# Moving the prompt's final mLSTM state from the mLSTM stage of a decoder step into the stage that chooses experts

## The chip, the cores and the metric

The kernel runs on one core of a Trainium2 chip. The metric is device time in microseconds (us); the time before is the median of three executions. The engines are TensorE (PE, matrix multiplication; PEld is its weight load), VectorE (DVE), ScalarE (ACT), GpSimd (POOL) and SyncE (SP), which here only issues transfers. Each engine runs its own instructions in order and waits on semaphores. Transfers run on 16 DMA engines, and each engine that issues transfers has a queue of its own on them: q1 in the profile carries what SP issues, q10 what ACT issues.

## What is computed

One inference step of one decoder layer, for a prompt of 256 tokens and 8 decoding sequences ("samples"), all in float32. The part that matters is the mLSTM with 4 heads of 256 x 256 and its final state for the prompt, then the mixture of experts.

```python
def mlstm_chunk(carry, inp):
    c0, n0, m0 = carry
    q, k, v, i_pre, logf = inp
    ...
    w_end = jnp.exp(F[..., -1:] + a - m_end[..., None])
    c1 = dec_end[..., None, None] * c0 + jnp.einsum('bhs,bhsv,bhsk->bhvk', w_end, v, k)
    n1 = dec_end[..., None] * n0 + jnp.einsum('bhs,bhsk->bhk', w_end, k)
    return (c1, n1, m_end), h
...
h = rmsnorm(x + concat([mlstm, attention]) @ w_out)
# each token: 1 of 4 groups, then 2 of its 8 experts
y = (silu(x_e @ w_gate[e]) * (x_e @ w_up[e])) @ w_down[e]     # 32 experts, 12 MB of weights each
```

`c1` (the memory, prompt_C, 4 heads of 256 KB) and `n1` (the normaliser, prompt_n, 4 rows of 1 KB) of the prompt are outputs. Nothing later in the step reads them.

## The kernel before

The work is laid out by hand in stages. Input projection, attention and mLSTM share one stream of weight chunks of 1 MB (`load_chunk`, `project_chunk`, line 154): the mLSTM stage (`mlstm`) issues 16 such chunks, `project(0)` to `project(15)`, on TensorE and puts the mLSTM's own small matmuls between them. Then comes the choosing stage (`route`): the rest of the output projection, logits, ranks, the gathering of the tokens of expert 0 (`gather_slots`, line 1292), and then `experts`, which takes the 32 experts in order.

The final state before. `weighted_values(h)` on VectorE writes `vw`, the values times `w_end`, for one head; `outer(h)` on TensorE (line 966) multiplies them with the keys in `ktok` into a PSUM bank; `copy_state(h)` on VectorE copies it to `cout`; SP stores it (`prompt_state`, line 869). `normaliser(j)` (line 975) does the same for `n1` with one column of weights, ScalarE copies the row (line 1097) and SP stores it. `outer` and `normaliser` stand between the chunks 7 and 11.

The weights of an expert are six items of 2 MB in a ring of six slots: items 0 and 1 are w_gate, 2 and 3 w_up, 4 and 5 w_down. Slots 0 to 2 are the tile `raw`, slots 3 to 5 the tile `more`; the queue SP loads slot `at` of the next expert when TensorE has used it (`chunk_used`). In `route`, SP loads expert 0 as its slots come free (3, 4, 5, 2, 0, 1), and two more items of expert 1 into other tiles ("extra", line 1476). Slot 2 is `core.raw[:, 4:6]`, and `ktok` and the buffer `hh` of the mLSTM stage are these same two parts of `raw`.

For an expert (line 1879) TensorE does `project(0, 0)`, `project(0, 1)` with slots 0 and 1, `project(1, 0)` with slot 2, `folded(0)`, `project(1, 1)` with slot 3, `folded(1)`, the gathering for the next expert, `down` with slots 4 and 5, and `x_turn`; the first four experts are followed by a piece of another projection (`ple_project`, lines 1333 and 1338). `folded(m)` waits for ScalarE's copy of the PSUM bank (lines 1762 and 1768, `gu_copied`). Ahead of its first such copy ScalarE runs `routing["after"]` (line 1569).

## Time and profile before

| | us |
|---|---|
| median of 3 executions | 1639.27 (1638.75 to 1639.69) |
| span of the profiled execution, first to last instruction | 1635.1 |
| difference of the median to that span | 4.2 |
| TensorE busy | 1355.8 (83%) |
| VectorE, ScalarE, GpSimd busy | 293.3, 226.8, 75.6 |
| traffic | 535.71 MB, mean 328 GB/s |

The profiled execution has no time of its own beside its span. Its parts by time: projections and attention to 313 us, the mLSTM stage from 313 to 459 us, the choosing stage from 459 to 547 us, the experts from 547 to 1478 us, the final stage to 1635 us. A row of the timeline is start, duration, engine, line, operation, output and inputs, count, and in square brackets the idle time of the engine ahead of it with what ended it. A matmul of 32-bit numbers counts as two records on PE.

### The profile page before, as it was taken

The page shows a single profiled execution, that of the slowest core. Times are in us where ns is not written, and L with a number is a line of the kernel's source. Part 1 is how long each engine was busy: PE and PEld are TensorE (multiplying, and loading weights), DVE is VectorE, ACT ScalarE, POOL GpSimd, SP SyncE. Part 2 cuts the span into 40 slices and gives each one's busy share as a digit, 9 for nine tenths or more (in the row PEclk, how much of TensorE's full clock was granted, in tenths as well). Part 3 has the DMA queues.
Part 4 walks back from the last instruction along what each step waited for, and adds up shares of the span by engine and source line. Part 5 has one row for each costly group of instructions (what it writes and reads, how often), then busy time and mean ns, then how long its engine had stood idle before and what let it go on. Part 6 is the DMA issues. An engine that isn't in the chain of part 4 may idle for free.

```text
span 1635.1 us, 21890 instructions
## 1 busy us (share of the span) xinstructions
PE 1355.8 (83%) x9071; PEld 754.3 (46%) x9072; DVE 293.3 (18%) x819; ACT 226.8 (14%) x512; POOL 75.6 (5%) x160
## 2 busy tenths in 40 slices
PE   9999999999999798777777767767677677676997
PEld 7878888888887333222222222222222222223543
DVE  4312321156512301010000100100100000103212
ACT  3101221223211111000000000000000000002303
POOL 1000000200040000000000000000000000000000
PEclk9999999999999799888978988888988887987999
DMA  9555333578886899999999999999999999996352
GB/s 314 176 178 182 129 129 120 185 255 319 266 297 253 357 427 427 428 428 428 428 428 429 428 428 429 427 429 428 428 429 429 428 428 418 425 392 211 105 178 80
DMA packets 106372, 535.71 MB, mean 328 GB/s; under 512 B 13988, under 2 KB 36712, under 8 KB 79945
## 3 DMA queue, kind: packets, MB, share of 16 engines
q1 hardware_dynamic: 101584, 530.56, 81.1%
q0 software_dynamic: 2560, 4.34, 0.7%
q8 instruction: 38, 0.62, 0.2%
q10 hardware_dynamic: 2176, 0.09, 0.1%
q14 instruction: 14, 0.11, 0.0%
HBM read 514.32 MB, written 24.62 MB: 330 GB/s over the span
## 4 chain that ended last, share of the span: by engine, by line
DMA 47%; PE 23%; DVE 1%; ACT 0%; issue 0%; SPq 0%; POOLq 0%; DVEq 0%
DMA raw<-in_w_up 38%; DMA more<-in_w_up 8%; PE ps L2081 7%; PE ps L1854 7%; PE ps L154 4%; PE ps L1292 1%; PE ps L2098 1%; PE ps L1874 1%; PE ps L1333 1%; PE ps L1863 1%; PE ps L1834 1%; DMA more<-expert_rows 0%; DMA expert_rows<-hT,si 0%; PE ps L1493 0%; PE ps L2070 0%
## 5 line engine op out<-in xcount | busy, mean ns | idle before, releaser
L1854 PE MATMUL ps<-raw,hT 128*32 128x512 f32 x1504 | 232.7, 752 | 158.7 <-DMA raw<-in_w_gate 95.6
L154 PE MATMUL ps<-hT,raw 128*128 128x264 f32 x1280 | 291.4, 387 | 0.0
L154 PEld LDWEIGHTS ps<-hT,raw 128*128 128x128 f32 x1280 | 240.8, 190 | 41.9 <-issue 1.5
L1854 PEld LDWEIGHTS ps<-raw,hT 128*32 128x32 f32 x1504 | 46.6, 125 | 310.7 <-DMA raw<-in_w_gate 124.5
L154 PE MATMUL ps<-mixT,raw 128*128 128x264 f32 x640 | 145.5, 387 | 2.4 <-PEq L839 1.5
L1874 PE MATMUL ps<-more,hid 128*32 128x512 f32 x1024 | 125.6, 620 | 21.1 <-DMA more<-in_w_down 21.0
L154 PEld LDWEIGHTS ps<-mixT,raw 128*128 128x128 f32 x640 | 120.8, 190 | 25.0 <-issue 3.9
L1863 PEld LDWEIGHTS ps<-fold,hT 128*128 128x128 f32 x512 | 69.6, 208 | 97.6 <-ACT hT L1768 61.7
L2081 PE MATMUL ps<-raw,more 128*128 128x512 f32 x256 | 114.1, 602 | 0.0
L1810 DVE TENSOR_TENSOR hid<-ps,sig 128x128 f32<-128x128 f32 x32 | 9.3, 291 | 573.3 <-PE ps L1863 573.3
L1292 PE MATMUL ps<-x_res,mine 128*32 128x512 f32 (+1 forms) x792 | 105.5, 649 | 2.2 <-DVE mine L1282 2.2
L1854 PE MATMUL ps<-more,hT 128*32 128x512 f32 x512 | 79.6, 751 | 32.8 <-DMA more<-in_w_up 32.7
L1863 PE MATMUL ps<-fold,hT 128*128 128x32 f32 x512 | 76.7, 295 | 22.9 <-ACT hT L1768 22.9
L1874 PEld LDWEIGHTS ps<-more,hid 128*32 128x32 f32 x1024 | 28.5, 113 | 118.5 <-issue 75.6
L1834 PEld LDWEIGHTS ps<-ident,xe 128*64 128x64 f32 x1056 | 66.8, 217 | 28.5 <-issue 28.5
L1762 ACT ACTIVATE hT<-ps 128x512 f32<-128x512 f32 x32 | 19.1, 597 | 411.4 <-PE ps L1854 411.4
L2081 PEld LDWEIGHTS ps<-raw,more 128*128 128x128 f32 x256 | 48.6, 193 | 57.8 <-issue 57.8
L1834 PE MATMUL ps<-ident,xe 128*64 128x64 f32 x1056 | 71.4, 288 | 0.8 <-ACT xe L1300 0.8
L1818 DVE COPY hT<-ps 128x512 f32<-128x512 f32 x32 | 22.1, 692 | 227.6 <-PE ps L1874 227.6
L1932 POOL DMA_INDIRECT expert_rows<-hT,si x32 | 31.5, 984 | 655.0 <-DVE hT L1818 655.0
L1292 PEld LDWEIGHTS ps<-x_res,mine 128*32 128x32 f32 (+1 forms) x792 | 19.8, 112 | 57.1 <-issue 55.7
L1854 PEld LDWEIGHTS ps<-more,hT 128*32 128x32 f32 x512 | 15.3, 124 | 61.4 <-DMA more<-in_w_up 35.6
(389 smaller groups left out, 793.4 us busy)
## 6 DMA issues: line engine op xcount, KB each, us to landing
more<-in_w_down SPq DMA_DIRECT2D x64, 2048.0 KB, 26.3
raw<-in_w_gate SPq DMA_DIRECT2D x62, 2048.0 KB, 26.3
more<-in_w_up SPq DMA_DIRECT2D x32, 2048.0 KB
raw<-in_w_up SPq DMA_DIRECT2D x32, 2048.0 KB, 26.6
raw<-in_w_in SPq DMA_DIRECT2D x44, 1024.0 KB, 5.1
raw<-in_w_out SPq DMA_DIRECT2D x16, 1024.0 KB, 8.5
raw<-in_w_ple_gate SPq DMA_DIRECT2D x16, 1024.0 KB, 5.0
x_res<-in_state_mlstm_C SPq DMA_DIRECT2D x8, 1024.0 KB, 8.4
```

Source lines behind the costliest of these rows:

```text
L154: return nc.tensor.matmul(ps[:, j, 0:NT], core.raw[:, q % NCH, k * GW + j * P:k * GW + (j + 1) * P], xT[:, core.groups[g].k0 + c * CK + k, ...
L1292: last = nc.tensor.matmul(ps[a * SLOTS:(a + 1) * SLOTS, 2, :], rt["mine"][0:n, t, :], core.x_res[0:n, t, a * GW:(a + 1) * GW], start=(t == ...
L1333: last = nc.tensor.matmul(ps[:, bank[t], :], core.pinT[:, k, t * P:(t + 1) * P], core.wp[:, k, g * GW:(g + 1) * GW], start=(k == 0), stop= ...
L1762: nc.scalar.activation(gu[:, 0, :], ps[:, GATE, :], ACT.Copy).then_inc(q["gu_copied"], 1)
L1818: V.tensor_copy(yq[:], ps[:, YB, :]).then_inc(q["y_copied"], 1)
L1834: last = nc.tensor.matmul(ps[h * 64:(h + 1) * 64, XB, k * 64:(k + 1) * 64], by_row[:, k, :], quarters[:, h], start=True, stop=True)
L1854: last = nc.tensor.matmul(ps[own, (GATE, UP)[m], :], xT[:, k, i * SLOTS:(i + 1) * SLOTS], weights, start=(i == 0 and k < 4), stop=(i == EI ...
L1863: last = nc.tensor.matmul(ps[:, GB, (m * 4 + j) * SLOTS:(m * 4 + j + 1) * SLOTS], gu[:, m, :].rearrange("p (i r k) -> p i k r", i=EI, k=2) ...
L1874: last = nc.tensor.matmul(ps[a * SLOTS:(a + 1) * SLOTS, YB, :], hid[:, 2 * i + k, :], chunk(2 * EI + i)[:, k * D + a * GW:k * D + (a + 1) ...
L1932: pool.indirect_dma_start(out=y4, out_offset=bass.IndirectOffsetOnAxis(ap=si[:, 0:1], axis=0), in_=yq[:], in_offset=None, bounds_check=8 * ...
L2081: last = nc.tensor.matmul(ps[:, 2 * t + g % 2, :], xT[:, c * CK + k, t * P:(t + 1) * P], core.raw[:, c, k * GW:(k + 1) * GW], start=(c == ...
L2098: last = nc.tensor.matmul(ps[a * SLOTS:(a + 1) * SLOTS, 4 + g % 2, 0:P], xsT[:, k, :], core.raw[:, k // CK, k % CK * GW + a * P:k % CK * G ...
```

## The change

The four `outer` and two `normaliser` groups, the copies and the stores leave the mLSTM stage. At its end VectorE writes all eight weighted value tiles into the buffer `hh` (now read as `vw` by `route`) and copies the weights to `core.end_cols`. In `route`, TensorE multiplies head by head (`state(h, b)`) at four places, and the normaliser after the gathering for expert 0, with its four heads in four column groups of the array. ScalarE copies the results to four places in the tile `hT` (`cout`) and to four rows of `pps`, and issues the eight stores itself. SP loads slot 2 for expert 0 (`item(2)`) only after the matmuls have read it. VectorE, GpSimd and ScalarE wait until all eight stores have landed (`r_cstored`, `state_stored`) before they reuse those places: ScalarE at the start of `after`.

```diff
@@ mlstm, tensor
-            project(7)
-            outer(0)
-            project(8)
+            for n in range(7, 12):
+                project(n)
             pe.wait_ge(q["m_den"], 2 * MH)
             pe.wait_ge(q["m_tab2T"], 2)
-            normaliser(0)
-            normaliser(1)
-            outer(1)
-            project(9)
-            outer(2)
-            project(10)
-            outer(3)
-            project(11)
-            pe.wait_ge(q["m_cout"], MH)
-            pe.wait_ge(q["m_nn"], 2)
@@ mlstm, vector, last
+            def weighted_values():
+                dve.wait_ge(q["m_hT"], 8)
+                V.tensor_copy(core.end_cols[:], cols[:, 2])
+                for h in range(MH):
+                    for b in range(2):
+                        V.tensor_scalar(hh[:, b, h, :], vaug[:, b, h, 0:DK], cols[:, 2, b, h:h + 1], None, ALU.mult)
@@ route, sync
         load_chunk(core, sp, first + NCH + 3)
-        item(2)
...
+        sp.wait_ge(q["r_state"], MH)
+        sp.wait_ge(q["r_nT"], 1)
+        item(2)
         sp.wait_ge(shared["xs_clear"], 1)
@@ route, tensor
+        def state(h, b):
+            for v in range(2):
+                last = nc.tensor.matmul(ps[:, state_bank[h], v * DK:(v + 1) * DK], vw[:, b, h, v * P:(v + 1) * P],
+                                        ktok[:, b, h * DK:(h + 1) * DK], start=(b == 0 and v == 0),
+                                        stop=(b == 1), skip_group_check=True)
+            if b == 1:
+                last.then_inc(q["r_state"], 1)
+        def normaliser():
+            for b in range(2):
+                for h in range(MH):
+                    last = nc.tensor.matmul(ps[32 * h:32 * h + 1, 3, 0:DK], core.end_cols[:, b, h:h + 1],
+                                            ktok[:, b, h * DK:(h + 1) * DK], start=(b == 0), stop=(b == 1))
+            last.then_inc(q["r_nT"], 1)
...
+        state(0, 0)
         pe.wait_ge(q["r_const"], 1)
         pe.wait_ge(q["r_l_copied"], 1)
...
         last.then_inc(q["r_pin_turned"], 1)
+        state(0, 1)
+        state(1, 0)
+        state(1, 1)
+        pe.wait_ge(q["r_pin_copied"], 1)
+        state(2, 0)
+        state(2, 1)
         pe.wait_ge(q["r_rank"], 1)
...
+        state(3, 0)
+        state(3, 1)
         gather_slots(core, pe, rt, shared, 0)
+        pe.wait_ge(q["r_c"], 1)
+        normaliser()
@@ route, scalar
+        for h in range(MH):
+            act.wait_ge(q["r_state"], h + 1)
+            nc.scalar.activation(cout[h], ps[:, state_bank[h], :], ACT.Copy).then_inc(q["r_c"], 1)
         slots_copy(core, act, rt, shared, 0)
...
+        act.wait_ge(q["r_nT"], 1)
+        for h in range(MH):
+            nc.scalar.activation(tail["pps"][32 * h:32 * h + 1, 0:DK], ps[32 * h:32 * h + 1, 3, 0:DK], ACT.Copy).then_inc(q["r_n"], 1)
+        act.wait_ge(q["r_c"], MH)
+        for h in range(MH):
+            act.dma_start(out["prompt_C"][0, 0, h].rearrange("(v p) k -> p v k", p=P),
+                          cout[h].rearrange("p (v k) -> p v k", v=2)).then_inc(q["r_cstored"], 16)
+        act.wait_ge(q["r_n"], MH)
+        for h in range(MH):
+            act.dma_start(out["prompt_n"][0, :, h, :], tail["pps"][32 * h:32 * h + 1, 0:DK]).then_inc(q["r_cstored"], 16)
     def after(act):
+        act.wait_ge(q["r_cstored"], 32 * MH)
         act.wait_ge(q["r_wts"], 1)
@@ experts, vector, body
                     slot_index(core, dve, rt, q, p)
+                    dve.wait_ge(*routing["state_stored"])
@@ experts, gpsimd, body
+                    pool.wait_ge(*routing["state_stored"])
                     link(nc.gpsimd.memset(tail["ybs"], 0.0))
```

TensorE's rows in the mLSTM stage, from chunk 7 on, before (L154 are the chunks, L966 `outer`, L975 `normaliser`, L984 the turning of the heads):

```order
L154 MATMUL ps<-hT,raw 128x264 x16
L966 MATMUL ps<-raw,vw 128x256 x4
L154 MATMUL ps<-mixT,raw 128x264 x16
L975 MATMUL ps<-raw,cols 1x256 x8
L966 MATMUL ps<-raw,vw 128x256 x4
L154 MATMUL ps<-mixT,raw 128x264 x16
L966 MATMUL ps<-raw,vw 128x256 x4
L154 MATMUL ps<-mixT,raw 128x264 x16
L966 MATMUL ps<-raw,vw 128x256 x4
L154 MATMUL ps<-mixT,raw 128x264 x16
L984 MATMUL ps<-ident,raw 128x128 x8
```

The same place after the change, from one group further up (L935 is `values`, L944 the turning of the heads):

```order
L935 MATMUL ps<-vaug,gain_row 128x257 x3
L154 MATMUL ps<-hT,raw 128x264 x16
L154 MATMUL ps<-mixT,raw 128x264 x64
L944 MATMUL ps<-ident,raw 128x128 x8
L154 MATMUL ps<-mixT,raw 128x264 x16
```

Chunks 7 to 11 now follow each other with nothing between them: 16 matmuls of `outer` and 8 of `normaliser` are gone from there.

ScalarE's rows at the end of the choosing stage and in expert 0, before (L1300 copies the gathered tokens, L1563 and L1565 are exponentials, L1569 is `after`, L1762 the copy for which `folded(0)` waits):

```order
L1300 ACTIVATE xe<-ps 128x512
L1563 ACT_TABLE_LOAD
L1563 ACTIVATE ra<-ra 128x12
L1565 ACTIVATE rc<-rc 128x3
L1569 ACTIVATE wts<-ps 128x2
L1762 ACTIVATE hT<-ps 128x512
```

and after the change (L1529, L1537 the new copies, L1540, L1544 the new stores, L1742 the copy for `folded(0)`):

```order
L1529 ACTIVATE hT<-ps 128x512 x4
L1231 ACTIVATE xe<-ps 128x512
L1532 ACT_TABLE_LOAD
L1532 ACTIVATE ra<-ra 128x12
L1534 ACTIVATE rc<-rc 128x3
L1537 ACTIVATE pps<-ps 1x256 x4
L1540 DMA out_prompt_C<-hT 128x2x256 x4
L1544 DMA out_prompt_n<-pps 1x256 x4
L1549 ACTIVATE wts<-ps 128x2
L1742 ACTIVATE hT<-ps 128x512
```

Eight copies and eight stores came in, and between the last store and L1549 stands the wait for all eight to have landed.

## Rows read from the trace of the kernel before

**Rows 1.** Page, the chain that ended last, by line.

```profile
DMA raw<-in_w_up 38%; DMA more<-in_w_up 8%; PE ps L2081 7%; PE ps L1854 7%; PE ps L154 4%; PE ps L1292 1%; PE ps L2098 1%; PE ps L1874 1%; PE ps L1333 1%; PE ps L1863 1%; PE ps L1834 1%; DMA more<-expert_rows 0%; DMA expert_rows<-hT,si 0%; PE ps L1493 0%; PE ps L2070 0%
```

**Rows 2.** Windows: stretch, length, busy per engine, clock, DMA share, GB/s.

```profile
380.00:459.00 79.00, 76.36 (x353) 62.97 (x351) 40.88 (x155) 24.60 (x57) 0.00 (x0) 1.00 0.84 291
544.00:546.00 2.00, 1.50 (x25) 1.53 (x26) 0.00 (x0) 1.95 (x4) 0.00 (x0) 0.95 0.97 395
546.00:552.00 6.00, 5.14 (x36) 1.67 (x37) 1.61 (x7) 0.00 (x0) 0.00 (x0) 0.50 0.06 14
552.00:560.00 8.00, 7.44 (x106) 3.10 (x98) 1.25 (x5) 2.71 (x5) 0.19 (x1) 0.96 0.98 383
```

**Rows 3.** Timeline of PE in the mLSTM stage, chunks 7 to 11.

```profile
379.03 7.28 PE L154 MATMUL ps<-hT,raw 128*128 128x264 f32 x32
386.15 1.89 PE L966 MATMUL ps<-raw,vw 128*128 128x256 f32 x8
...
395.09 3.62 PE L975 MATMUL ps<-raw,cols 128*1 128x256 f32 x16
...
407.58 1.89 PE L966 MATMUL ps<-raw,vw 128*128 128x256 f32 x8
...
418.26 1.97 PE L966 MATMUL ps<-raw,vw 128*128 128x256 f32 x8 [1.67 <-DVE vw L1139]
...
427.18 1.04 PE L984 MATMUL ps<-ident,raw 128*128 128x128 f32 x8
```

**Rows 4.** Timelines of DVE and PE, the samples' last values and their user.

```profile
444.12 0.23 DVE L1240 TENSOR_TENSOR nsq<-num 128x64 f32<-128x64 f32 x1
...
450.30 0.53 PE L1041 MATMUL ps<-nsq,ones 128*128 128x32 f32 x4
```

**Rows 5.** Timeline of PE, end of choosing stage and experts 0, 1.

```profile
528.80 0.77 PE L1521 MATMUL ps<-logit_fold,space 128*128 128x36 f32 x6 [1.38 <-DVE space L1595]
...
535.60 0.80 PE L1529 MATMUL ps<-both,upper 128*128 128x128 f32 x2 [4.99 <-DVEq L1624]
...
539.24 4.45 PE L1292 MATMUL ps<-x_res,mine 128*32 128x512 f32 x24 [2.19 <-DVE mine L1282]
544.50 2.21 PE L1834 MATMUL ps<-ident,xe 128*64 128x64 f32 x32 [0.81 <-ACT xe L1300]
...
554.61 1.92 PE L1854 MATMUL ps<-raw,hT 128*32 128x512 f32 x16
556.46 1.13 PE L1863 MATMUL ps<-fold,hT 128*128 128x32 f32 x8
...
564.06 3.64 PE L1874 MATMUL ps<-more,hid 128*32 128x512 f32 x32
...
577.25 1.90 PE L1854 MATMUL ps<-raw,hT 128*32 128x512 f32 x16
```

**Rows 6.** DMA view of 436 to 440 us: SP's queue, and the stores.

```profile
q1 hardware_dynamic: 546, 0.53, 38.1%
...
out_prompt_C<-cout SPq DMA_DIRECT2D x2, 256.0 KB, 2.8
```

**Rows 7.** DMA view of 11 to 20 us: queue, packets, MB, share of 16 engines.

```profile
q1 hardware_dynamic: 1577, 3.13, 98.4%
q10 hardware_dynamic: 1547, 0.05, 12.2%
```

**Rows 8.** DMA view of 800 to 1000 us, SP's queue.

```profile
q1 hardware_dynamic: 5818, 84.77, 99.5%
```

**Rows 9.** Timelines of SP and ACT at expert 0.

```profile
551.27 2.82 SPq L1716 DMA_DIRECT2D raw<-in_w_gate  x2
...
554.78 0.59 ACT L1762 ACTIVATE hT<-ps 128x512 f32<-128x512 f32 x1
```

**Rows 10.** Timeline of PE in the final stage, after an idle stretch.

```profile
1494.06 5.62 PE L2081 MATMUL ps<-raw,more 128*128 128x512 f32 x8
...
1499.95 3.60 PE L2081 MATMUL ps<-raw,more 128*128 128x512 f32 x8
```

More of the change, by code:

```diff
@@ L811, in mlstm @@
     skq = spare[0:NS, 0:2 * MH * DK].rearrange("p (i c) -> p i c", i=2)
-    nout = spare[0:1, 2 * MH * DK:3 * MH * DK].rearrange("p (h k) -> p h k", h=MH)
     vaug = S("vaug", [P, 2, MH, DK + 1])
     kq = S("kq", [P, 2, 2, MH * DK])
-    vw = S("vw", [P, 2, DK])
-    cout = S("cout", [P, 2, 2, DK])
     n0 = S("n0", [NS, MH, DK])
@@ L912, in _ @@
                 load_chunk(core, sp, n)
-            for i in range(2):
-                sp.wait_ge(q[f"m_cst{i}"], 16 * (MH // 2))
-            sp.wait_ge(q["m_stored"], 64)
+            sp.wait_ge(q["m_stored"], 48)
             sp.wait_ge(q["m_cstored"], 16 * NS)
@@ L955, in values @@
                 last.then_inc(q["m_num"], 1)
-            def outer(h):
-                if h == 0:
-                    pe.wait_ge(q["m_wt"], MH)
-                if h >= 2:
-                    pe.wait_ge(q["m_cout"], h - 1)
-                for b in range(2):
-                    pe.wait_ge(q["m_vw"], 2 * h + b + 1)
-                    for v in range(2):
-                        last = nc.tensor.matmul(ps[:, 4 + h % 2, v * DK:(v + 1) * DK], vw[:, b, v * P:(v + 1) * P],
-                                                ktok[:, b, h * DK:(h + 1) * DK], start=(b == 0 and v == 0),
-                                                stop=(b == 1), skip_group_check=True)
-                last.then_inc(q["m_c"], 1)
-            def normaliser(j):
-                for h in (2 * j, 2 * j + 1):
-                    for b in range(2):
-                        last = nc.tensor.matmul(ps[0:1, 6 + j, (h % 2) * DK:(h % 2 + 1) * DK], cols[:, 2, b, h:h + 1],
-                                                ktok[:, b, h * DK:(h + 1) * DK], start=(b == 0), stop=(b == 1))
-                last.then_inc(q["m_nT"], 1)
             def heads(j):
@@ L1094, in _ @@
             decay(4)
-            for j in range(2):
-                act.wait_ge(q["m_nT"], j + 1)
-                nc.scalar.activation(nout[:, 2 * j:2 * j + 2, :], ps[0:1, 6 + j, :].rearrange("p (h c) -> p h c", h=2),
-                                     ACT.Copy).then_inc(q["m_nn"], 1)
             partial(0)
@@ L1353, in ple_copy, with route @@
         nc.scalar.activation(dst, src, ACT.Copy).then_inc(shared["pp_copied"], 1)
-def route(core, w, part, mixT, rt, shared, ctx):
+def route(core, w, out, part, mixT, rt, shared, ctx):
     nc, ps = core.nc, core.ps
@@ L1393, in route @@
     first = core.first_chunk[first_group]
+    vw = core.raw[:, NCH, :].rearrange("p (b h k) -> p b h k", b=2, h=MH)
+    ktok = core.raw[:, NCH + 1, :].rearrange("p (b c) -> p b c", b=2)
+    flat = part[:].rearrange("p k t -> p (k t)")
+    cout = [flat[:, c:c + 2 * DK] for c in (1536, 2560, 3072, 3584)]
+    state_bank = (3, 7, 1, 4)
     def pool(pool):
@@ L1657, in vector @@
         dve.sem_inc(q["r_wt"], 1)
-    return {"pool": pool, "sync": sync, "tensor": tensor, "scalar": scalar, "vector": vector, "extra": extra, "tables": tables, "after": after, "wp_landed": q["r_wp"],
+    return {"pool": pool, "sync": sync, "tensor": tensor, "scalar": scalar, "vector": vector, "extra": extra, "tables": tables, "after": after, "wp_landed": q["r_wp"], "state_stored": (q["r_cstored"], 32 * MH),
             "pin_copied": q["r_pin_copied"], "free": oT}
@@ L2333, in build @@
             shared = dispatch_sems(core)
-            routing = route(core, w, hT, mixT, rt, shared, s)
+            routing = route(core, w, out, hT, mixT, rt, shared, s)
             last = tail_stage(core, w, rt, routing["free"], ydram, out["y_prompt"], out["y_sample"])
```

39 lines of the change are left out of this document (5 added, 34 removed).

## The prediction

> **What bounds the kernel now.** I read the chain that ended last first [rows 1]: nearly half of it is "DMA in_w_up", the wait for expert weights, and the rest is TensorE. So there are two regimes, and a change has to be judged at the border. The windows give it [rows 2]: in the mLSTM stage (380 to 459 us) TensorE is busy 76.4 of 79 us; in 552 to 560 us the 16 DMA engines are busy 0.98 and stay so through the experts (in 800 to 1000 us SP's queue alone fills 99.5%, 84.77 MB [rows 8]). From 552 us on, the end is therefore "traffic still to be moved, plus gaps". One load of 2 MB costs 2.097 MB / (84.77 MB / 200 us) = 4.95 us there. Just ahead of it lies a hole: in 546 to 552 us the DMA engines are busy 0.06 and in 544 to 546 us 0.97, so 5.7 us are idle, because every slot is full until expert 0 has used slot 0 (SP's next load is issued at 551.27 [rows 9]). A microsecond saved on TensorE ahead of 546 us moves everything behind it by one; anything after that counts only if it adds traffic or opens a gap in it.
>
> I keep the clock of the kernel before for all times below and subtract the first saving at the end.
>
> **Step 1, what leaves the mLSTM stage.** From the first `outer` at 386.15 to the turning of the heads at 427.18 are 41.03 us [rows 3]. They hold four chunks; a chunk takes 386.15 - 379.03 = 7.12 us. So 41.03 - 4 x 7.12 = 12.5 us go: four `outer` groups of 1.9 us, the normaliser's 3.6 us and a stall of 1.67 us on a weighted value. Do the other engines follow? The tightest follower is VectorE, whose samples' values end at 444.35 for a matmul at 450.30 [rows 4], 5.9 us of slack. The steps ahead of them are paced by ScalarE behind the chunks and move along; VectorE also loses its waits on stores. Its eight new weighted values come after its last step, beside TensorE's last chunk of 7.12 us; at about 0.4 us each (an estimate; a copy of twice the size takes ScalarE 0.59 [rows 9]) they are hidden there. DMA is busy 0.84 of 79 us [rows 2], 66.4 us, less 3.0 us for the stores that leave (0.381 x 4 us for two of them is 1.52 us [rows 6]): 63.4 us of work in 66.5 us. That is tight but fits, and a chunk's load is issued as soon as the chunk four ahead of it is used. I take **-12.5 us**, bounds -11 and -12.5 with a stall.
>
> **Step 2, the matmuls in the choosing stage.** `state(0, 0)` is half an `outer`, 0.95 us, in a wait of 1.38 us ahead of 528.80; `state(0, 1)` to `state(2, 1)` are 4.7 us in a wait of 4.99 us ahead of 535.60; `state(3)` is 1.9 us in one of 2.19 us ahead of 539.24 [rows 5]. All are covered, just. The normaliser's 16 records follow the gathering. Before, in one column group, 16 cost 3.6 us [rows 3]; the gathering runs 24 records of twice the columns in four groups in 4.45 us at the low clock [rows 5], so four groups cost 4.45 x 16/24/2 = 1.5 us, against a wait of 0.81 us for the gathered tokens: at most 0.7 us late on `x_turn`. In the other direction, the granted clock in 546 to 552 us is 0.50, the level of 1.2 GHz [rows 2], after TensorE had waited three times; filled waits may keep the 2.4 GHz and save some 3 us on the gathering and the first two projections. Neither decides anything, as step 3 shows: behind 546 us the queue, not TensorE, is full. I count 0.
>
> **Step 3, what the DMA engines get to do at the border.** Slot 2's load (4.95 us) used to run earlier in the choosing stage, beside TensorE's chunks; it is now issued at about 543 to 546 us, after the normaliser. The four stores add 3.0 us in the same place. Both fall in the hole of 5.7 us, so the traffic is +7.95 - 5.7 = +2.3 us longer there, if nothing else waits.
>
> **Step 4, the new wait of ScalarE.** In order behind it stand the copy of `wts`, then the copy of expert 0's gate bank at 554.78 [rows 9], for which `folded(0)` waits at 556.46 [rows 5], and behind that all of expert 0 and every free slot after the third. So I need the moment when the eight stores have landed. On an idle queue one store lands 2.8 us after its issue [rows 6], and issued at 546 to 549 us they would be just in time. But they are on ACT's queue q10 while SP's q1 is full. How two queues share shows at the start of the kernel: in 11 to 20 us q1 moved 1577 packets and q10 1547, one for one, though q1's were 2 KB and q10's 32 bytes, and q1 filled the engines all the while [rows 7]. The turn is by packet, not by size. A store here is 256 packets of 1 KB (546 packets for two stores and little else [rows 6]), four are 1024 or 64 per engine. Expert weights are 84.77 MB / 5818 = 14.6 KB per packet [rows 8], in the main 16 KB, 8 per load and engine. So each 1 KB of state waits for 16 KB of weights. From 546.2 us q1 holds slot 2, then slots 0 and 1 of expert 2 and slot 2 of expert 1, as TensorE frees them up to `project(1, 0)`: 4 x 8 = 32 packets per engine, fewer than 64. The stores thus get half of their turns, q1 runs dry because TensorE stands at `folded(0)`, and the rest rushes through: landed at 546.2 + 4 x 4.95 + 3.0 = **569 us**. With ScalarE's two copies TensorE goes on at about 570.5, 14 us later than 556.46.
>
> The Trainium skill (DMA: Bandwidth & Descriptors, section "Queues, rings and completion order") says that a DMA engine round-robins between queues packet by packet, a packet being some 9 to 17 descriptors. The trace agrees on the one-for-one turn; if the turn is a store's 16 rows against a load's 8, the four stores still need four loads' time, and the same 569 us comes out.
>
> **Step 5, the gaps.** After 14 us idle TensorE restarts slowly, as at 1494.06, where 8 records take 5.62 us instead of 3.60 [rows 10]; I give `folded(0)` and `project(1, 1)` (1.13 + 1.92 us) 5.7 us. Slot 3 is free at 576.2, and 0.8 us pass from issue to traffic (551.27 to 552 [rows 2, 9]): DMA idle 569.0 to 577.0, **8.0 us**. That load ends at 581.9; slot 4 is free after ScalarE's copy (0.6 and a pass 0.1), `folded(1)` 1.1, gathering 2.9 and half of `down` 1.8 [rows 5], at 582.7: idle **1.6 us**. Slots 4 and 5 fill to 593.4. Slot 2 of expert 1 is free 577.25 + 1.90 - 561.2 = 17.9 us after the end of `folded(1)` [rows 5], at 595.9: idle **3.3 us**. After that loads stay ahead. Gaps 12.9 us against the old hole of 5.7.
>
> **Sum.** -12.5 + 4.95 + 3.0 + 12.9 - 5.7 = +2.7 us. On the profiled span 1635.1 that is 1637.8, with the 4.2 us outside it **1642 us**. The saving is real and is given back at the border.
>
> **Rivals.**
> - *The stores get through at once.* If q10 may move several packets per turn against one of 16 KB, or the shares go by bytes, they land by about 552, ScalarE is hardly late, and only step 3 remains: -12.5 + 2.3 = -10.2, 1629 us. For it: 3.0 us of traffic is little; 2.8 us landing on an idle queue. Against: 1577 to 1547.
> - *Partly.* Two or three packets per turn: landed at 558 to 563. Up to about 558 the loads already queued cover ScalarE's lateness; each later us costs about one. 1632 to 1638, say 1636 us.
> - *Slower, by the mLSTM stage.* 63.4 us of traffic in 66.5 us leaves nothing for order: if the samples' state loads, which wait for stores to land, come over 5.9 us late at the matmul of 450.30, part of the 12.5 is lost there, besides step 4. With 5 us lost: 1647 us. Against: the last of these loads has some 9 us to spare by my reckoning.
>
> **How the numbers follow.** About 0.2%, 3.3 us, is what can be told from no change here. The forecast with stores held back has 0.70; its own range is 1638 to 1648 (restart at full clock -2.3, landing later or the low clock lasting longer +3, step 1 up to +1.5, slower normaliser +0.5), of which I put 0.38 within 0.2% and 0.32 beyond it on the slow side. Stores at once 0.15, all faster. Partly 0.07, 0.05 faster and 0.02 same. The mLSTM stall 0.08, slower. So faster 0.20, same 0.40, slower 0.40. The range 1632 to 1649 leaves out the bulk of "at once" and little above.
>
> **What would show it.** In the profile after: the choosing stage starts at 446.5 instead of 459.0 (step 1); `x_turn` at its place in the stage within 1 us (step 2); DMA engines busy with no hole from the extra loads to the end of the stores (step 3); ScalarE's copy for `folded(0)` about 16 us later within the stage, and TensorE idle there for 14 to 17 us, with q10 carrying some 1100 packets spread over 20 us (step 4); DMA gaps of 8, 1.6 and 3.3 us after (step 5); the steady waits for expert weights shifted about 3 us later in spite of step 1. I am wrong if ScalarE goes on within 5 us of issuing, if the gaps are under 8 us in all, or if TensorE waits for chunks or samples ahead of the choosing stage.

## The result, and the profile after

The changed kernel takes 1646.15 us (median of 4, 1641.82 to 1647.44) beside 1639.48 us before (median of 4): ratio 1.004, 95% interval 1.0023 to 1.0057. In a later comparison on another occasion it took 1643.49 us (11 executions) beside 1640.57, ratio 1.0019 (1.0007 to 1.0031). So it is slower by 0.2 to 0.4%. The profiled execution of after has a span of 1640.1 us, 5.0 more than that of before; it took 1641.82 us, the fastest of the four.

The page of after, the chain that ended last, by line, and one piece of the chain in order of time (start, duration):

```profile
DMA raw<-in_w_up 46%; PE ps L2063 7%; PE ps L1835 6%; PE ps L154 4%; DMA out_prompt_n<-pps 1%; PE ps L1223 1%; PE ps L2080 1%; PE ps L1855 1%; PE ps L1844 1%; PE ps L1264 1%; DMA more<-expert_rows 0%; PE ps L1815 0%; DMA expert_rows<-hT,si 0%; PE ps L1431 0%; PE ps L2052 0%
```

```profile
536.32 22.23 DMA out_prompt_n<-pps
```

The chain is that of before [rows 1] but for one link: a store of the normaliser, whose four stores are 4 KB in all, now stands in it for 22.23 us. ScalarE waits for all eight stores; this is the one that the profile puts last, and the records of the other four, 1 MB, are most of what its queue carries in that time.

The timeline of TensorE at the start of the choosing stage, before:

```profile
459.50 21.60 PE L154 MATMUL ps<-mixT,raw 128*128 128x264 f32 x96 [1.47 <-PEq L839]
```

and after, from there to the first gathering of the experts (columns: start, duration, and in square brackets the idle time ahead of the group and what ended it; the first row is cut off by its window):

```profile
447.05 5.13 PE L154 MATMUL ps<-mixT,raw 128*128 128x264 f32 x22 [1.39 <-PEq L836]
...
514.90 1.13 PE L1448 MATMUL ps<-raw 128*128 128x256 f32 x4
...
518.10 4.58 PE L1448 MATMUL ps<-raw 128*128 128x256 f32 x20
...
524.16 1.92 PE L1448 MATMUL ps<-raw 128*128 128x256 f32 x8
526.41 2.92 PE L1223 MATMUL ps<-x_res,mine 128*32 128x512 f32 x24 [0.33 <-DVE mine L1213]
529.25 1.04 PE L1458 MATMUL ps<-raw,end_cols 128*1 128x256 f32 x16
530.24 2.14 PE L1815 MATMUL ps<-ident,xe 128*64 128x64 f32 x32
...
541.75 2.50 PE L1835 MATMUL ps<-raw,hT 128*32 128x512 f32 x16 [3.89 <-DMA raw<-in_w_up]
559.28 1.91 PE L1844 MATMUL ps<-fold,hT 128*128 128x32 f32 x8 [15.03 <-ACT hT L1742]
561.13 3.64 PE L1835 MATMUL ps<-more,hT 128*32 128x512 f32 x16
565.49 1.92 PE L1844 MATMUL ps<-fold,hT 128*128 128x32 f32 x8 [0.72 <-ACT hT L1748]
567.34 4.34 PE L1223 MATMUL ps<-x_res,mine 128*32 128x512 f32 x24
```

Three things are to be read here. The choosing stage starts at 447.05 where it started at 459.50 before: 12.45 us are saved ahead of it. The state's products (L1448) and the normaliser (L1458) fit in the waits: the gathering at 526.41 comes 12.83 us earlier than at 539.24 [rows 5], the turning of the tokens 14.3 us earlier than at 544.50. Then TensorE stands for 15.03 us ahead of the first folding (L1844), and the folding takes 1.91 us, where it took 1.13 us before [rows 5].

The wait of ScalarE on its timeline, with the stores that ACT's queue issues:

```profile
531.32 0.42 ACTq L1540 DMA_DIRECT2D out_prompt_C<-hT  x1
...
534.03 2.59 ACTq L1544 DMA_DIRECT2D out_prompt_n<-pps  x4
558.57 0.17 ACT L1549 ACTIVATE wts<-ps 128x2 f32<-128x2 f32 x1 [25.49 <-DMA out_prompt_n<-pps]
```

What the queues did, from the DMA view of 545 to 549 us and of 556 to 559 us (packets, MB, share of the 16 engines):

```profile
q1 hardware_dynamic: 108, 1.59, 92.8%
q10 hardware_dynamic: 107, 0.10, 7.2%
...
q10 hardware_dynamic: 211, 0.19, 18.4%
q1 hardware_dynamic: 5, 0.02, 1.3%
```

While SP's queue has weights, one 1 KB record of the state moves for each record of 16 KB: 108 on q1 to 107 on q10, and 102 to 102 and 112 to 114 in the 4 us ahead of this window and behind it. (In 537 to 541 us, when q1 also carried the small records of the sample rows, it was 243 to 306.) When q1 runs dry, at about 556 us, q10 gets rid of its last 211 records within 3 us.

The windows of the kernel after (the last three columns are granted clock, DMA share and GB/s):

```profile
543.00:558.00 15.00, 1.25 (x8) 0.00 (x0) 0.00 (x0) 0.00 (x0) 0.00 (x0) 0.50 0.90 377
558.00:571.00 13.00, 11.00 (x52) 4.91 (x56) 1.20 (x4) 2.82 (x5) 1.14 (x2) 0.53 0.41 152
571.00:580.00 9.00, 9.00 (x79) 4.25 (x72) 1.90 (x4) 0.60 (x1) 1.21 (x1) 1.00 0.65 244
580.00:616.00 36.00, 34.56 (x311) 14.36 (x313) 3.08 (x8) 6.07 (x13) 1.34 (x3) 1.00 0.93 380
```

The idle time of the DMA engines is length times (1 - share): 1.5 + 7.7 + 3.1 + 2.5 = 14.8 us. Before, these engines had no gap behind the border, only the hole of 5.7 us ahead of it [rows 2].

### The profile page after: what moved, and what is told of

The parts are those of the page before. It is cut to its first block, busy times and chain, and to the rows that moved or that the text cites. A ratio compares the mean times of both kernels' runs of the same rounds, so it can differ in the third digit from the quotient of the medians.

```text
span 1640.1 us, 21891 instructions
## 1 busy us (share of the span) xinstructions
PE 1360.9 (83%) x9071; PEld 755.9 (46%) x9072; DVE 290.8 (18%) x816; ACT 230.0 (14%) x518; POOL 75.6 (5%) x160
## 3 DMA queue, kind: packets, MB, share of 16 engines
q0 software_dynamic: 2560, 4.34, 0.7%
## 4 chain that ended last, share of the span: by engine, by line
DMA 48%; PE 22%; DVE 1%; ACT 1%; issue 0%; ACTq 0%; SPq 0%; POOLq 0%; DVEq 0%
DMA raw<-in_w_up 46%; PE ps L2063 7%; PE ps L1835 6%; PE ps L154 4%; DMA out_prompt_n<-pps 1%; PE ps L1223 1%; PE ps L2080 1%; PE ps L1855 1%; PE ps L1844 1%; PE ps L1264 1%; DMA more<-expert_rows 0%; PE ps L1815 0%; DMA expert_rows<-hT,si 0%; PE ps L1431 0%; PE ps L2052 0%
## 5 line engine op out<-in xcount | busy, mean ns | idle before, releaser
L154 PE MATMUL ps<-hT,raw 128*128 128x264 f32 x1280 | 291.4, 387 | 0.0
L154 PEld LDWEIGHTS ps<-hT,raw 128*128 128x128 f32 x1280 | 240.8, 190 | 41.9 <-issue 1.5
L154 PE MATMUL ps<-mixT,raw 128*128 128x264 f32 x640 | 145.0, 387 | 2.4 <-PEq L836 1.4
L154 PEld LDWEIGHTS ps<-mixT,raw 128*128 128x128 f32 x640 | 120.8, 190 | 25.0 <-issue 3.8
L1844 PEld LDWEIGHTS ps<-fold,hT 128*128 128x128 f32 x512 | 72.6, 216 | 116.5 <-ACT hT L1748 63.4
L1844 PE MATMUL ps<-fold,hT 128*128 128x32 f32 x512 | 79.9, 303 | 37.9 <-ACT hT L1748 22.8
L1742 ACT ACTIVATE hT<-ps 128x512 f32<-128x512 f32 x32 | 19.1, 598 | 409.0 <-PE ps L1835 409.0
```

What stands on the lines that cost most here:

```text
L154: return nc.tensor.matmul(ps[:, j, 0:NT], core.raw[:, q % NCH, k * GW + j * P:k * GW + (j + 1) * P], xT[:, core.groups[g].k0 + c * CK + k, ...
L1742: nc.scalar.activation(gu[:, 0, :], ps[:, GATE, :], ACT.Copy).then_inc(q["gu_copied"], 1)
L1844: last = nc.tensor.matmul(ps[:, GB, (m * 4 + j) * SLOTS:(m * 4 + j + 1) * SLOTS], gu[:, m, :].rearrange("p (i r k) -> p i k r", i=EI, k=2) ...
```

## The experiments

Three measures are used. One is the median with its ratio to the kernel before, which ran beside each. The second is taken from the trace: the time from the first gathering for expert 0 to the first products of the final stage with the weights (1494.06 in [rows 10]). It holds the border and all experts, and leaves out the stages ahead, whose length varies between executions (last section). Before it is 1494.06 - 539.24 = 954.8 us, after 1500.05 - 526.41 = 973.6. The third is the idle time of the DMA engines in the four windows shown for the kernel after, shifted for each kernel with its first gathering (16.6 to 89.6 us behind it).

| Kernel | Median, us | Ratio to before (95%) | Gathering to final stage, us | DMA gaps, us |
|---|---|---|---|---|
| before | 1638.4 to 1640.6 | 1 | 954.8 | none |
| after | 1646.15 | 1.004 (1.0023 to 1.0057) | 973.6 | 14.8 |
| after, again | 1643.49 | 1.0019 (1.0007 to 1.0031) | 976.6 | 17.4 |
| left_out | 1624.14 | 0.9911 (0.9891 to 0.993) | 952.7 | none |
| no_stores | 1623.63 | 0.9916 (0.9893 to 0.9939) | 954.7 | 0.2 |
| sp_queue | 1629.79 | 0.9946 (0.9925 to 0.9967) | 958.5 | 1.0 |
| late_wait | 1639.68 | 1.0006 (0.9994 to 1.0018) | 969.5 | 11.9 |
| one_head | 1629.02 | 0.9936 (0.992 to 0.9953) | 959.0 | 0.5 |
| sp_late | 1628.05 | 0.9923 (0.9907 to 0.9939) | 959.4 | none |
| norm_one | 1629.17 | 0.9942 (0.9922 to 0.9962) | 958.3 | none |
| busy_wait | 1650.37 | 1.0069 (1.0051 to 1.0087) | 978.8 | 19.8 |
| busy_half | 1641.74 | 1.0017 (0.9998 to 1.0037) | 971.2 | 10.0 |
| wide_rows | 1646.85 | 1.0045 (1.003 to 1.006) | 976.6 | 16.9 |
| sp_wide | 1627.69 | 0.9931 (0.9911 to 0.995) | 956.1 | none |

The 954.7 us of no_stores plus 3.0 us for the stores' own traffic plus the gaps give the stretch of every other kernel with stores in it to 2.0 us, busy_half alone to 3.5. So this loss is gaps in the traffic, and differences of under 2 us in the stretch are not read below.

**left_out: what the mLSTM stage alone is worth.** No products, copies and stores of the state; slot 2's load stands where it stood before.

```diff
-        state(0, 0)
...
-        pe.wait_ge(q["r_c"], 1)
-        normaliser()
...
         load_chunk(core, sp, first + NCH + 3)
+        item(2)
```

> This kernel leaves the prompt's final memory and normaliser out altogether (no matmuls, copies or stores of them), and loads slot 2 at its old place; it is step 1 alone. Theory (the saving is whole in the mLSTM stage and is given back only at the border to the experts): 12.4 us under before, 1627 us, with the hole of 5.7 us between the extra loads and slot 0's reload as before. Rival (the time ahead of the border is hidden by something behind it): within 3 us of before.

Measured: 952.7 us, which is 2.1 less than before, and 1624.14 us. The ratio makes 0.0089 x 1639.5 = 14.6 us, more than the 12.45 us of the mLSTM stage by about what the stretch is shorter. The saving comes through to the end entirely, and the rival falls.

**no_stores: the new place of slot 2's load.** All of the change but the eight stores and ScalarE's wait for them.

```diff
-        act.wait_ge(q["r_c"], MH)
-        for h in range(MH):
-            act.dma_start(out["prompt_C"][0, 0, h]...
...
     def after(act):
-        act.wait_ge(q["r_cstored"], 32 * MH)
```

> This kernel does all of the change but the eight stores (the two outputs stay unwritten) and ScalarE's wait for them. Theory (the wait for stores that share the DMA engines packet by packet with the weights costs the time): slot 2's 4.95 us fall into the hole of 5.7 us, the matmuls into waits of TensorE, so 1627 us as without the state at all, 1 us more at most; ScalarE's copy for the first folding directly after TensorE's third projection. Rival (the moved matmuls, the normaliser and the late slot 2 cost it): 1636 us or more.

The timeline of TensorE of this kernel at slot 2:

```profile
541.14 3.44 PE L1827 MATMUL ps<-raw,hT 128*32 128x512 f32 x16 [3.60 <-DMA raw<-in_w_up]
544.52 1.13 PE L1836 MATMUL ps<-fold,hT 128*128 128x32 f32 x8
```

Measured: 1623.63 us, and 954.7 us, just the 954.8 of before, though 4.95 us of traffic are new in this stretch. The load fills the hole, TensorE's new wait of 3.60 us for it costs nothing, and the folding starts straight after the projection. Against left_out it is 2.0 us more, and no difference in the median. So slot 2's move is no part of the loss that this can tell.

**sp_queue: the same stores on SP's queue.** C ahead of slot 2's load, n behind the sample rows.

```diff
+        sp.wait_ge(q["r_c"], MH)
+        for h in range(MH):
+            sp.dma_start(out["prompt_C"][0, 0, h]...
         sp.wait_ge(q["r_state"], MH)
         sp.wait_ge(q["r_nT"], 1)
         item(2)
```

> All of the change, but SP issues the eight stores: the four of the memory just ahead of slot 2's load, the four of the normaliser after the sample rows. Theory (turns between two queues): in SP's own queue they are served in order, the memory lands some 5 us after its turn comes and all of it by about 543 us of the span, ScalarE is late by 2 us at most; -12.4 + 7.95 - 5.7 = -10.2, 1629 us. Rival (1 KB stores under load are slow whatever the queue): landed at about 556 us again, 1640 us or more.

ScalarE's and TensorE's timelines:

```profile
545.70 0.17 ACT L1549 ACTIVATE wts<-ps 128x2 f32<-128x2 f32 x1 [10.99 <-DMA out_prompt_n<-pps]
...
547.43 3.64 PE L1835 MATMUL ps<-raw,hT 128*32 128x512 f32 x16 [7.93 <-DMA raw<-in_w_up]
551.00 1.45 PE L1844 MATMUL ps<-fold,hT 128*128 128x32 f32 x8
```

Measured: 958.5 us and 1629.79 us. ScalarE still waits 10.99 us for the stores, but is through before TensorE has slot 2. The wait of 15 us ahead of the folding is gone; in its place TensorE waits 7.93 us for slot 2's load instead of 3.89, with the DMA engines full. The bytes are those of the changed kernel, and it is 15.1 us shorter from gathering to final stage. This is the cause in one run: not the stores, but the queue they stand on.

**late_wait: a later wait.** Stores on ACT's queue as in after, but ScalarE waits for them only ahead of its first copy into that region, VectorE likewise. GpSimd's wait stays where it was.

```diff
     def after(act):
-        act.wait_ge(q["r_cstored"], 32 * MH)
...
                     expert(p, e, e)
+                    if e == 0:
+                        act.wait_ge(*routing["state_stored"])
                     ple_copy(core, act, q, e)
```

> All of the change with ScalarE's queue, but the wait for the stores stands later: ScalarE's ahead of the first copy of the other projection, VectorE's ahead of its copy of expert 0's result. Theory (one packet of weights for each packet of state, as long as SP's queue has any): TensorE now frees four more slots before anything waits, so the stores wait behind seven loads instead of four and land at 533.8 + 7 x 4.95 + 3 = 571 us of the span instead of 557; TensorE stands ahead of expert 1 instead of at the first folding; one gap of about 14 us instead of several, total about 1643 us. Rival (the stores take a fixed 25 us on that queue): landed at 557 us, nearly nobody waits, 1630 us.

ScalarE's timeline:

```profile
578.23 1.08 ACT L1284 ACTIVATE mixT<-ps 128x512 f32<-128x512 f32 x2 [19.55 <-DMA out_prompt_n<-pps]
```

Measured: 969.5 us, 1639.68 us. The folding is not held back any more (550.35 in a profile whose stages run 5 us later than in after), and the stores now land at 577.8 us. Taken 5 us earlier that is 572.8, where 571 was expected: the stores do not land after a fixed 25 us, but later when more loads stand in SP's queue. That the kernel would take 1643 us was wrong by 3 us. Waiting later helps only by 4 us in the stretch, since more loads get in between the stores' turns and the gap comes later (in 578 to 589 us the DMA engines are busy 0.13 of the time); it is 11.9 us in all.

**one_head: 16 turns per engine instead of 64.** Heads 0 to 2 of C on SP's queue, head 3 on ACT's. The four stores of n were to go to SP's queue too; the edit leaves them on ACT's.

```diff
-        for h in range(MH):
+        for h in (3,):
             act.dma_start(out["prompt_C"][0, 0, h]...
...
+        for h in range(3):
+            sp.dma_start(out["prompt_C"][0, 0, h]...
```

> SP's own queue issues the stores of heads 0 to 2 ahead of slot 2's load and those of the normaliser behind the sample rows that it loads; only head 3 of C (256 records of 1 KB, 16 per DMA engine) stays on ACT's queue; ScalarE's wait for all eight stores is where the changed kernel has it. Theory (record for record turns): 16 turns of 0.62 to 0.66 us, one with each 16 KB packet, take 10 to 11 us from about 534 to 535 us: head 3 lands at about 545 us, so ScalarE's copy for the first folding is late by 2 us at most, and q10 carries some 256 packets in place of 1096. 1630 us, 1628 to 1633. Rival (anything that stands on ACT's queue lands only when SP's queue has run dry, whatever its size): landing near 557 us as in the changed kernel, TensorE waits some 12 us at the folding, 1640 us or more.

Timelines of ScalarE and TensorE:

```profile
545.14 0.17 ACT L1553 ACTIVATE wts<-ps 128x2 f32<-128x2 f32 x1 [10.19 <-DMA out_prompt_n<-pps]
...
547.60 3.38 PE L1839 MATMUL ps<-raw,hT 128*32 128x512 f32 x16 [7.85 <-DMA raw<-in_w_up]
```

and the queues in 537 to 541 us:

```profile
q1 hardware_dynamic: 500, 1.51, 94.3%
q10 hardware_dynamic: 262, 0.26, 18.6%
```

Measured: all eight stores landed by 545.14 us, 280 records on q10, 959.0 us, 1629.02 us. The rival that anything on ACT's queue lands at 557 us falls. That it was 11 us as reckoned is chance, and no test of the turns against 16 KB records: 262 of the 280 records moved within 4 us, beside 500 of q1, many of them SP's own stores of 1 KB records, and in sp_queue, with no store on ACT's queue, ScalarE went on at 545.70 us as well.

**sp_late and norm_one: order of the stores, and the normaliser's column groups.** In sp_late all stores stand behind slot 2's load on SP's queue, with the late waits of late_wait (GpSimd's wait is not moved, though the expectation says so):

```diff
         item(2)
+        sp.wait_ge(q["r_c"], MH)
+        for h in range(MH):
+            sp.dma_start(out["prompt_C"][0, 0, h]...
```

norm_one is sp_late with the records of each head one after the other, in two column groups (its normaliser also waits for three copies of ScalarE instead of one):

```diff
-            for b in range(2):
-                for h in range(MH):
-                    last = nc.tensor.matmul(ps[32 * h:32 * h + 1, 3, 0:DK], ...
+            for h in range(MH):
+                for b in range(2):
+                    last = nc.tensor.matmul(ps[h // 2 * 32:h // 2 * 32 + 1, 3, (h % 2) * DK:(h % 2 + 1) * DK], ...
```

> All eight stores on SP's queue, those of C behind slot 2's load; ScalarE waits for their landing only ahead of the first copy into the state's region after the first down projection, VectorE and GpSimd as late. Theory (after the border only traffic counts, and no gap is opened): what is left of the change is the mLSTM stage's -12.4 us, and against it slot 2's load in the hole and the stores, as in the run with the stores on SP's queue ahead of the load: 1629 us, 1627 to 1632, and within 0.1% of that run; TensorE waits some 3 to 4 us for slot 2's load instead of 8. Rival (TensorE's progress at the border still counts, since the order of the stores decides when slot 2 is there): 4 us better than that run, 1625 to 1626 us.

> The kernel with all stores behind slot 2's load on SP's queue, with the normaliser's 16 records in order of heads, so that records of one column group of 32 follow each other (two groups, one after the other) instead of four groups in turn. From rows of the kernel before, 16 records in one group took 3.6 us; the four groups in turn took 1.04 us in the changed kernel. Theory: the normaliser takes 3 to 3.6 us here, some 2.3 us more, and the turning of the picked tokens starts about as much later; the end moves by under 1 us, since behind the border traffic sets it, except that slot 2's load is issued 2.3 us later, where the queue has run dry: 1629 to 1631 us. Rival: the four groups make no difference at full clock (1.0 to 1.5 us either way).

TensorE's row of the normaliser in norm_one:

```profile
529.64 2.75 PE L1465 MATMUL ps<-raw,end_cols 128*1 128x256 f32 x16
```

Measured: sp_late takes 959.4 us against 958.5 of sp_queue; TensorE waits 4.16 us for slot 2 instead of 7.93, and the stretch is no shorter for it, as the first theory has it. The medians are 1628.05 and 1629.79 us with overlapping intervals; less than 2 us can't be excluded. The normaliser takes 2.75 us, less than the 3 to 3.6 expected, against 1.04 in four groups in turn; a gain of 1.7 us of TensorE, which the end doesn't show (958.3 us, intervals of the medians overlap).

**after_again.** The changed kernel unaltered, once more.

> The changed kernel unaltered, beside the others on one chip. Theory (stores held back on ACT's queue, gaps of some 15 us behind it): slower than the kernel before by 1 to 8 us, 1641 to 1647 us, and 11 to 17 us over the kernel with the stores on SP's queue behind slot 2's load. Rival (the earlier difference of 6.7 us came mostly from scatter between executions): 1640 us, within 1 us of the kernel before.

Measured: 1643.49 us, 2.9 over the kernel before and 15.4 over sp_late beside it. In the two profiles of this kernel ScalarE waits 25.49 and 25.58 us. Two rows of the second, the gathering behind the restart and the window that matches 571 to 580 us of the first:

```profile
572.73 5.50 PE L1223 MATMUL ps<-x_res,mine 128*32 128x512 f32 x24
...
576.30:585.30 9.00, 9.00 (x77) 3.38 (x73) 0.69 (x1) 0.60 (x1) 0.18 (x1) 0.73 0.35 117
```

The low clock lasted longer here: the gathering took 5.50 us instead of 4.34, the clock in this window was 0.73 instead of 1.00 and the DMA engines' share 0.35 instead of 0.65. The gaps are 17.4 us instead of 14.8, and the stretch is 3.0 us longer. So the loss itself varies between executions, with the low clock.

**busy_wait and busy_half: what the low clock adds.** TensorE is kept busy in its two waits with products that nobody reads, so that the clock doesn't fall; the stores stay as in after.

```diff
+                for i in range(14 if idle else 0):      # 28 in busy_wait
+                    nc.tensor.matmul(ps[:, 5, 0:P], core.ident[:], core.ones[:], start=True, stop=True)
                 project(1, 0, n)
+                for i in range(58 if idle else 0):      # 104 in busy_wait
+                    nc.tensor.matmul(ps[:, 5, 0:P], core.ident[:], core.ones[:], start=True, stop=True)
                 folded(0, n)
```

> The changed kernel, in which TensorE runs 28 products of the identity with ones (128 columns, into a bank that nobody reads) in its wait for slot 2 and 104 in its wait ahead of the first folding, some 0.13 us each at full clock: 3.6 and 13.5 us in waits of 3.9 and 15.0 us. The stores land as before. Theory (the term of the gaps was undersized because the low clock lasted over the whole restart): the granted clock stays at 1.00, folding, projection, folding and gathering take 1.13, 1.92, 1.13 and 2.91 us instead of 1.91, 3.64, 1.92 and 4.34, the DMA gaps shrink from 14.9 us to 10 to 11, and from the first gathering of slots to the first product of the final stage there are 969 to 970 us instead of 973.6: about 4.5 us less, 1638 to 1640 us beside 1643.5. Rival (the gaps come from the wait alone, and later loads catch up on the slow restart): within 1 us of the changed kernel, 973 us. Rival 2: the clock falls all the same.

Measured: 1650.37 us. The products were sized wrongly: a product leaves two records of 0.113 us, 208 records took 23.49 us, and the folding came 10 us later than in after. Still, 978.8 us is only 5.2 more than 973.6; the run doesn't decide between the theory and the first rival. The clock stayed up (the second folding took 1.13 us), so rival 2 falls.

> The filled waits once more, at half the number of products: each product left two records of 0.113 us, not one, so that 104 products ran past the wait by 10 us in the last run. Now 14 in the wait for slot 2 (3.3 of 3.9 us) and 58 ahead of the first folding (13.1 of some 14 to 15 us). The stores land as in the changed kernel. Theory (low clock over the restart costs 4.7 us, which the gaps pass on to the end): folding, projection, folding and gathering at full clock, 969 to 970 us from the first gathering of slots to the first product of the final stage instead of 973.6 to 976.6, 4 to 5 us less than the changed kernel. Rival (gaps come from the wait alone): 973 to 976 us, the changed kernel's time.

TensorE's timeline of busy_half at the restart, and its windows:

```profile
544.42 13.22 PE L1872 MATMUL ps<-ones,ident 128*128 128x128 f32 x116
560.14 1.13 PE L1844 MATMUL ps<-fold,hT 128*128 128x32 f32 x8 [2.51 <-ACT hT L1742]
561.20 1.92 PE L1835 MATMUL ps<-more,hT 128*32 128x512 f32 x16
...
564.90 2.91 PE L1223 MATMUL ps<-x_res,mine 128*32 128x512 f32 x24
```

```profile
545.00:560.00 15.00, 12.64 (x114) 12.45 (x112) 0.36 (x1) 0.57 (x2) 0.54 (x1) 1.00 0.83 345
560.00:570.00 10.00, 9.14 (x80) 3.78 (x84) 0.84 (x4) 2.85 (x5) 0.59 (x2) 1.00 0.57 208
570.00:580.00 10.00, 10.00 (x96) 4.88 (x92) 1.90 (x4) 1.26 (x3) 1.21 (x1) 1.00 0.93 371
580.00:590.00 10.00, 9.28 (x84) 3.67 (x76) 0.58 (x2) 1.47 (x3) 0.18 (x1) 1.00 0.80 300
590.00:616.00 26.00, 25.28 (x225) 10.25 (x224) 2.49 (x6) 3.92 (x8) 1.16 (x2) 1.00 0.99 411
```

The clock stays at 1.00, the four groups take 1.13, 1.92, 1.13 and 2.91 us, and the DMA engines are idle for 2.5 + 4.3 + 0.7 + 2.0 + 0.3 = 9.8 us up to 616 us (10.0 in the table's windows), where after had 14.8. At the end 971.2 us are left of 973.6 and 976.6, and 1641.74 us of 1643.5 to 1646: 2 to 5 us less where 4 to 5 were expected. Where the rest goes shows at the last expert, whose third projection waits for its weights (after, then busy_half):

```profile
1465.62 3.64 PE L1835 MATMUL ps<-raw,hT 128*32 128x512 f32 x16 [1.85 <-DMA raw<-in_w_up]
...
1461.23 1.92 PE L1835 MATMUL ps<-raw,hT 128*32 128x512 f32 x16 [1.80 <-DMA raw<-in_w_up]
```

From the first gathering these are 939.2 and 934.1 us: all 5 us are still there. From there to the final stage after takes 34.4 us and busy_half 37.1. So the low clock is a third of the gaps and reaches the last expert whole; the stretch behind it, which varied from 33.4 to 37.1 us in all kernels here, hides 2.7 us of it in this execution.

**wide_rows and sp_wide: records of 2 KB.** Rows 2r and 2r + 1 of C on one partition, so that a store is 128 records of 2 KB.

```diff
-    nc.tensor.matmul(ps[...], vw[:, b, h, v * P:(v + 1) * P], ktok...
+    nc.tensor.matmul(ps[...], vw[:, b, h, :].rearrange("p (r v) -> p v r", v=2)[:, v], ktok...
...
-    act.dma_start(out["prompt_C"][0, 0, h].rearrange("(v p) k -> p v k", p=P), cout[h]...
+    act.dma_start(out["prompt_C"][0, 0, h].rearrange("(p v) k -> p (v k)", v=2), cout[h]).then_inc(q["r_cstored"], 16)
```

> The changed kernel with the stores still on ACT's queue, but rows 2r and 2r+1 of each head's C on partition r, so that a store is 128 records of 2 KB instead of 256 of 1 KB (the left operand of the state's products is taken with stride two). Theory (a turn is one record, whatever its size, against one record of 16 KB): the four stores need 32 turns per DMA engine instead of 64, at 0.62 to 0.70 us each 20 to 22 us from 533.5: landed at 554 to 555 instead of 557 us, just when SP's queue runs dry, so that about the last 3 us of the delay go; q10 carries 512 fewer records; SP's queue stands still for 3 to 4 us instead of 9. From the first gathering to the final stage 966 to 970 us instead of 973.6, 1635 to 1639 us. Rival (shares go by bytes, or the stores wait until the other queue is dry whatever their number): landed at 557, no change in time.

DMA view of wide_rows in 545 to 549 and 549 to 553 us, and ScalarE's wait:

```profile
q1 hardware_dynamic: 109, 1.52, 89.0%
q10 hardware_dynamic: 107, 0.19, 12.2%
...
q1 hardware_dynamic: 104, 1.59, 92.7%
q10 hardware_dynamic: 58, 0.10, 6.6%
```

```profile
559.71 0.17 ACT L1548 ACTIVATE wts<-ps 128x2 f32<-128x2 f32 x1 [24.96 <-DMA out_prompt_n<-pps]
```

The expectation failed (976.6 us instead of 966 to 970). Half as many records (584 on q10 instead of 1096) land at 559.7 us in a profile that runs 1.7 us later, only 0.5 us earlier than in after instead of 2 to 3. The turns were one for one up to 549 us, with twice the bytes in a turn; then q10 moves one record for two of q1. That would be so if half of the engines had no such record left, that is, if the 2 KB records lie unevenly on the 16 engines; the records don't show which engine each ran on, so this stays open. The kernel takes 1646.85 us, as after. Summed over the windows from 534 to 562 us, q10's records took 2.8 us of the 16 engines here and 3.0 us in after, so their size hardly changes their own traffic.

> The kernel with all stores behind slot 2's load on SP's queue and late waits, with the same records of 2 KB. Theory (on one queue in order, only the time that the stores occupy the engines counts; two stores of 256 KB in 1 KB records took 1.52 us, 345 GB/s, where weights in 16 KB records move at 424): 0.4 to 0.6 us less, which is about what a measurement tells at best: 1627 to 1628.5 us. Rival (small records cost far more beside or behind large ones than on an idle queue): 2 us or more less, since the kernels with stores on SP's queue take 958.3 to 959.4 us from the first gathering to the final stage, against 954.7 without stores: 4 us for 3.0 us of traffic.

Measured: 956.1 us, 3.3 less than sp_late, but 1627.69 us against 1628.05 in medians, with ratios that overlap. The gain expected from their own traffic is below what this can tell; what the records' size is worth on one queue isn't settled, at most some 3 us.

## Why the prediction was right

Time and sign came out within the range, and the forecast mechanism is the one that the runs show. The size was less exact: the forecast was +2.7 us, and the two comparisons gave +6.7 and +2.9. By its steps:

**Step 1** held: -12.45 us against -12.5 (the stage started at 459.50 before, not at 459.0). VectorE's weighted values took 2.19 us, behind its last step and beside a chunk, and nothing else came late.

**Step 2** held, with its side branch: the waits filled, the granted clock stayed at 1.00 up to 543 us (0.50 in 546 to 552 before [rows 2]), the gathering took 2.92 us instead of 4.45 [rows 5] and the normaliser 1.04 us where 1.5 was the estimate. The tokens were turned 1.8 us earlier within the stage. That the moved matmuls keep the clock up is shown by left_out, which lacks them: TensorE waits 2.19 us there as before, and the gathering takes 4.95 us:

```profile
528.35 4.95 PE L1223 MATMUL ps<-x_res,mine 128*32 128x512 f32 x24 [2.19 <-DVE mine L1213]
```

That a microsecond or two of TensorE decides nothing there is shown by norm_one and sp_late.

**Step 3** held: with no_stores the 4.95 us of slot 2's load vanish in the hole (954.7 against 954.8). With all on one queue, sp_queue, the stretch is 3.7 us longer than before; 4.95 + 3.0 - 5.7 = 2.3 was the sum.

**Step 4** held to 1.5 us. Subtracting the 12.5 us, the stores were to land at 556.5 and TensorE to go on at 558.0; ScalarE went on at 558.57 and TensorE at 559.28, after 15.03 us idle (14 forecast). q10 carried 1096 records in 23 us, from 535 to 558 us (some 1100 over 20 forecast). The landing doesn't depend much on the exact turn, since the sum took the time at which all that is queued has moved. The Trainium skill's page "DMA: Bandwidth & Descriptors", section "Queues, rings and completion order", says that an engine changes queues after a packet of several descriptors; the counts of 108 to 107 agree with an even exchange, and can't tell turns of one record from equal turns of several, since the 16 engines need not be in step. The prediction's variant, 16 rows of a store against 8 of a load, would be two to one, which the counts don't show.

**Step 5** is the term that was too small: gaps of 12.9 us forecast, 14.8 and 17.4 measured. The prediction gave the slow restart 2.7 us, on two groups, and these it had right (5.7 us for 1.91 + 3.64); the second folding and the gathering it took at full clock. The clock stayed at 0.50 from 543 us until about 570, over all four. Those took 1.91 + 3.64 + 1.92 + 4.34 us instead of 1.13 + 1.92 + 1.13 + 2.92, 4.7 us more. busy_half shows it: with the clock held up the idle time is 5 us shorter. The prediction's range named it ("the low clock lasting longer +3").

**The sum**: -12.4 + 4.95 + 3.0 + 14.8 - 5.7 = +4.7 us, against +5.0 between the two spans. That this is closer than 2 us is luck: the spans differ by -12.8 us up to the first gathering, +18.8 in the stretch, where the sum has 17.1, and -1.0 in the final stage.

**The base** had an error of its own. "The 4.2 us outside it" isn't there: in every execution of both kernels seen since, time less span is 1.7 to 2.1 us. The profiled execution of before was one of its quicker ones, about 1637 us, and the median is 2 us above it. Adding the +2.7 to the median gives 1642 again, so this error cost the forecast nothing.

**The rivals.** "At once" is what sp_queue does (1629 forecast, 1629.8 measured), so its price was right and its condition false. "Partly" did not occur either: the turns were even (108 to 107). one_head and sp_queue agree with its remark that the loads already queued cover some lateness: ScalarE went on at 545.14 and 545.70 us there, and no time was lost. The stall in the mLSTM stage did not occur: no wait for a chunk or a sample stands in TensorE's timeline there.

## What to carry to other kernels

Where a loop is bound by weight traffic that comes in large records, a small store on another queue is not small: count its records per DMA engine against those of the loads ahead, reckon when all that is queued has moved, and compare with the moment at which somebody waits for it. That gave the landing to 2 us in after and late_wait; for records of 2 KB it failed (wide_rows). Put such a store on the queue of the loads, in the order in which it is needed; here that turns a loss of 0.2 to 0.4% into a gain of 0.8% (sp_late, 1628.05 us, ratio 0.9923, interval 0.9907 to 0.9939), the best kernel of this study beside sp_wide. And behind a stall of 15 us TensorE came out at a granted clock of 0.50 for 11 us and more, and the loads waited for that too: 5 of the 14.8 us of gaps.

## What the runs showed of the hardware that had not been expected

**The scatter between executions starts in the first 30 us.** The window 15 to 20 us of the second profile of the changed kernel, and a row of TensorE from it:

```profile
15.00:20.00 5.00, 5.00 (x19) 2.87 (x19) 2.50 (x6) 2.37 (x8) 0.00 (x0) 0.50 1.11 353
```

```profile
38.08 2.00 PE L331 MATMUL ps<-mixT,wg 128*32 128x264 f32 x32
```

and the same window and row of the first profile of the same kernel:

```profile
15.00:20.00 5.00, 4.03 (x21) 2.98 (x21) 4.54 (x9) 4.41 (x8) 0.00 (x0) 1.00 1.11 353
```

```profile
33.16 1.99 PE L331 MATMUL ps<-mixT,wg 128*32 128x264 f32 x32
```

The granted clock falls to 0.50 there in some executions (also in late_wait's) and not in others, and where it falls this row is 4.9 us later and the gathering 5.3 (531.72 against 526.41). That is as much as the whole effect of this change, so the traces are compared here from a point behind it. What decides it is open. Another 3.0 us lie between the two profiles behind that point (976.6 against 973.6 us), with 2.6 us more of gaps at the border (after_again).

**Four stores of 256 KB took over 25 us to land** beside a full queue of large records (ScalarE waited 25.49 us for them), and one of them 2.8 us where its queue had little else [rows 6].

**Fewer, larger records landed hardly sooner** (wide_rows, 0.5 us), though the turns were one for one at first. The cause is open.
